# A hybrid diffusion trunk step on one core: layer 0's shift and scale modulation on 32-column tiles of TensorE, the gate sums moved among the Hyena projections, small loads on three queues

## The chip, the cores and the metric

One core of one Trainium2 chip runs the whole step in one launch. The metric is the device time of that launch in microseconds (us). Everything is computed in f32.

The engines are TensorE (PE; its weight loads are shown apart as PEld), VectorE (DVE), ScalarE (ACT), GpSimd (POOL) and SyncE (SP), which here only issues DMAs. ACT and POOL issue DMAs too, on queues of their own. A name such as SPq stands for the issuing side of an engine.

## What is computed

Two layers work on 640 tokens (512 latent tokens of one request, 128 context tokens of another), with a model width of 1024. Ahead of each layer stands the modulation that this change is about:

```
m = silu(cond) @ mod_w[i] + mod_b[i]          # cond: c or c_ctx, 1024 -> 3072
shift, scale, gate = split(m, 3)              # 1024 each
h = rms_norm(x, pre_norm_g[i]) * (1 + scale) + shift
x = x + gate * rms_norm(mixer(h), post_norm_g[i])
```

There are two conditioning vectors (`c` for latent tokens, `c_ctx` for context tokens), so that each layer multiplies two rows of 1024 by a matrix of 1024x3072. Shift and scale (columns 0 to 2047) are needed before the layer's input projection, the gate (columns 2048 to 3071) only after its output projection.

Layer 0's mixer runs a bidirectional gated DeltaNet (GDN) on one half of the channels and a Hyena long convolution on the other. The Hyena filters come from a small network (`hyena_ffn_w1`, `w2`, `w3`, with sines between) and are turned into spectra by matrix products with DFT tables. Layer 1 is attention; the change touches it only by where its modulation is computed.

## The kernel before

Every engine has a program written out by hand; each waits on semaphores. PSUM has 8 banks, used in a ring: each use is a numbered "fill", `FILLS` lists all of them in order, and fill f may be written when fill f-8 has been drained. `bank_full` counts fills that TensorE has completed, `bank_free` those that ScalarE or VectorE has drained.

**Weights.** All large weights come in chunks of 1024x256 (1 MB) into `wring`, which has `WSLOTS` = 3 slots. `chunk_list` gives the chunks in the order of their loads, `slot_of` the slot of each (before: chunk i in slot i mod 3), and SP issues them in that order (L563). It waits for each one's slot: chunk i may be loaded when the last fill computed with the chunk that had the slot before is full, which for a modulation chunk is the fill `mod_f` (below).

**Modulation.** A matrix of 1024x3072 is 12 chunks. Most chunks are summed on VectorE: `sum_modulation` (L1682, L1685) multiplies and adds the 8 row blocks of a chunk with the conditioning values as scalars, for both vectors: 16 instructions of 128x256. TensorE then adds over the 128 partitions with `modulation` (four products with a column of ones, 128x1), which makes the fill `mod_f`, and VectorE's `take_modulation` (L1696) adds the bias and drains it. Four of layer 0's chunks (1, 4, 7 and 10) go to TensorE alone: 16 products of 128x2. The sums have two places (`macc`).

**The stages around the change.**
1. Start: small loads on SP's queue (network weights, biases, frequencies, norm rows, `ident`), two layers of the filter network (TensorE, VectorE, ScalarE in turn), two transposes of the rows of vectors, SiLU of the conditioning.
2. Filters: 20 products of 128x512, each drained by VectorE.
3. Spectra: `spectrum` makes 24 fills with 42 products (L1102; two and two in 12 steps n), drained by ScalarE and VectorE (`take_spectra`). After each step n comes one modulation chunk of layer 0. ScalarE also squares and normalises x in the middle of this stage (L742, L793).
4. `turn_x` (L1199): x is transposed, and ScalarE (L803) and VectorE (L1751) apply scale and shift to it, into `hT`. For this all 12 chunks of layer 0 are needed, the gate's four included.
5. Hyena projections: eight times `project_cm` (`hy_f`, j = 0 to 7), each with one chunk of `even_in_w`: 16 products of 128x512 and 16 of 128x128. After each one from j = 1 on comes one modulation chunk of layer 1. ScalarE copies the result to `pad` (`take_rows`, L828), and VectorE's `convolve` (three taps) reads `pad` before the next may be copied there.
6. `tr_hy` (ten groups of four transposes, L1223, copied by VectorE at L1789), the DFT products `fft0`, and so on; then the six GDN projections `qkv_f` with five-tap convolutions. After q1, k0, k1, v0 and v1 stand the last five modulation chunks of layer 1.

## Time and profile before

| | |
|---|---|
| median of 3 runs | 1221.07 us (1217.9 to 1229.56) |
| the profiled execution's own time | 1225.3 us |
| its span, first to last instruction | 1223.5 us |
| mean granted TensorE clock over the span | 0.949 |
| TensorE busy | 1127.3 us (92%) |
| VectorE busy | 617.5 us (50%) |
| ScalarE, GpSimd busy | 308.0 us, 116.9 us |
| loads and stores | 78.99 MB |

The profiled execution is 4.2 us above the median of the runs. Start times in the rows count from the first instruction. Each f32 product stands in the trace as two records, so that "x8" at a `MATMUL` row is four products. The granted clock is 1.00 at 2.4 GHz and 0.50 at 1.2 GHz.

### The profile page before, as it was taken

The page shows a single profiled execution, that of the slowest core. Times are in us where ns is not written, and L with a number is a line of the kernel's source. Part 1 is how long each engine was busy: PE and PEld are TensorE (multiplying, and loading weights), DVE is VectorE, ACT ScalarE, POOL GpSimd, SP SyncE. Part 2 cuts the span into 40 slices and gives each one's busy share as a digit, 9 for nine tenths or more (in the row PEclk, how much of TensorE's full clock was granted, in tenths as well). Part 3 has the DMA queues.
Part 4 walks back from the last instruction along what each step waited for, and adds up shares of the span by engine and source line. Part 5 has one row for each costly group of instructions (what it writes and reads, how often), then busy time and mean ns, then how long its engine had stood idle before and what let it go on. Part 6 is the DMA issues. An engine that isn't in the chain of part 4 may idle for free.

```text
span 1223.5 us, 13372 instructions
## 1 busy us (share of the span) xinstructions
PE 1127.3 (92%) x5234; PEld 796.6 (65%) x5234; DVE 617.5 (50%) x1426; ACT 308.0 (25%) x751; POOL 116.9 (10%) x156
## 2 busy tenths in 40 slices
PE   3998999989899997899898889899999998999997
PEld 1456466567356555679698878788965655445686
DVE  3988235658396778856738810600028146333104
ACT  1064001000012135532121101611161356333212
POOL 2020000000120004110004300600000000010001
PEclk9997999998899898889899989899999999969999
DMA  8465142440010322010004111331221200000012
GB/s 272 127 205 174 35 132 75 137 136 2 1 35 18 126 72 70 1 35 1 1 1 138 50 72 35 96 95 61 69 69 45 70 1 0 1 1 1 1 35 86
DMA packets 68430, 78.99 MB, mean 65 GB/s; under 512 B 2606, under 2 KB 63518, under 8 KB 68368
## 3 DMA queue, kind: packets, MB, share of 16 engines
q1 hardware_dynamic: 64776, 69.54, 17.8%
q0 software_dynamic: 2304, 7.96, 2.1%
q8 instruction: 42, 0.69, 0.2%
q10 hardware_dynamic: 1288, 0.64, 0.2%
q14 instruction: 20, 0.16, 0.0%
HBM read 74.62 MB, written 3.51 MB: 64 GB/s over the span
## 4 chain that ended last, share of the span: by engine, by line
PE 73%; DVE 17%; ACT 4%; POOL 3%; issue 2%; DMA 1%; SPq 0%; POOLq 0%; DVEq 0%; ACTq 0%
PE ps L1102 69%; PE ps L1223 4%; DVE pad L1685 2%; DVE phase L1771 1%; DVE mix L1685 1%; DVE xreg L1771 1%; DVE xreg L2036 1%; DMA wring<-in_mod_w 1%; DVE phase L2044 1%; POOL stat L604 1%; DVE xreg L2058 1%; ACT phase L1072 1%; DMA phase<-in_hyena_sin_freq 1%; PE ps L1199 0%; DVE pad L1960 0%
## 5 line engine op out<-in xcount | busy, mean ns | idle before, releaser
L1102 PE MATMUL ps<-hT,wring 128*128 128x512 f32 (+2 forms) x1376 | 363.0, 425 | 2.3 <-ACT hT L803 2.3
L1102 PEld LDWEIGHTS ps<-hT,wring 128*128 128x128 f32 x1376 | 206.4, 192 | 157.5 <-issue 155.1
L1102 PE MATMUL ps<-phase 128*128 128x512 f32 (+4 forms) x518 | 173.3, 480 | 10.5 <-ACT phase L753 5.0
L1102 PE MATMUL ps<-wring,mix 128*128 128x256 f32 x640 | 140.2, 382 | 3.0 <-issue 2.2
L1102 PEld LDWEIGHTS ps<-phase 128*128 128x128 f32 (+2 forms) x518 | 86.8, 198 | 83.5 <-issue 67.1
L1102 PEld LDWEIGHTS ps<-wring,mix 128*128 128x128 f32 x640 | 122.5, 192 | 20.4 <-issue 2.6
L1102 PE MATMUL ps<-wring,hT 128*128 128x256 f32 (+1 forms) x480 | 100.4, 372 | 0.0
L1102 PEld LDWEIGHTS ps<-wring,hT 128*128 128x128 f32 x480 | 89.7, 192 | 10.6
L2084 DVE SCALAR_TENSOR_TENSOR phase<-phase,yst 128x1024 f32<-128x1024 f32 x10 | 12.9, 1287 | 124.2 <-POOL yst L604 124.2
L1223 PE MATMUL ps<-ident,phase 128*128 128x128 f32 x376 | 52.7, 297 | 20.2 <-DVE phase L1972 5.7
L1102 PE MATMUL ps<-hT,phase 128*128 128x64 f32 (+4 forms) x258 | 70.1, 408 | 0.8 <-DVE phase L1722 0.8
L1685 DVE SCALAR_TENSOR_TENSOR mix<-wring,scond,mix 128x256 f32<-128x256 f32 x168 | 67.5, 476 | 0.0
L1102 PE MATMUL ps<-xreg,phase 128*128 128x128 f32 (+1 forms) x420 | 57.2, 296 | 10.3 <-DVE xreg L2050 4.9
L1223 PEld LDWEIGHTS ps<-ident,phase 128*128 128x128 f32 x376 | 47.6, 155 | 26.7 <-issue 9.9
L1102 PEld LDWEIGHTS ps<-xreg,phase 128*128 128x128 f32 x420 | 49.4, 193 | 16.6 <-issue 9.2
L2099 DVE TENSOR_SCALAR ostat<-ostat 128x35 f32<-128x35 f32 x1 | 0.2, 180 | 109.6 <-ACT pad L997 109.6
L1102 PEld LDWEIGHTS ps<-hT,phase 128*128 128x128 f32 (+2 forms) x258 | 35.8, 196 | 27.5 <-issue 25.2
L962 ACT ACTIVATE phase<-ps 128x256 f32<-128x256 f32 x40 | 15.3, 382 | 122.0 <-PE ps L1102 122.0
L828 ACT ACTIVATE pad<-ps 128x512 f32<-128x512 f32 x24 | 14.1, 598 | 124.2 <-PE ps L1102 114.7
L1685 DVE SCALAR_TENSOR_TENSOR pad<-wring,scond,pad 128x256 f32<-128x256 f32 x112 | 44.9, 470 | 0.0
L1102 PE MATMUL ps<-mix,phase 128*128 128x64 f32 (+1 forms) x136 | 33.8, 418 | 5.4 <-DVE phase L1654 5.4
L2159 DVE TENSOR_REDUCE smax<-ps 128x1 f32<-128x512 f32 x32 | 22.0, 687 | 27.9 <-PE ps L1102 27.8
(302 smaller groups left out, 1247.0 us busy)
## 6 DMA issues: line engine op xcount, KB each, us to landing
wring<-in_mod_w SPq DMA_DIRECT2D x24, 1024.0 KB, 5.2
wring<-in_even_in_w SPq DMA_DIRECT2D x16, 1024.0 KB, 7.3
wring<-in_odd_in_w SPq DMA_DIRECT2D x9, 1024.0 KB, 5.2
wring<-in_even_out_w SPq DMA_DIRECT2D x4, 1024.0 KB, 7.4
wring<-in_odd_out_w SPq DMA_DIRECT2D x4, 1024.0 KB, 5.2
xreg<-in_x_sample SPq DMA_DIRECT2D x1, 2048.0 KB, 13.8
xreg<-in_x_sample POOLq DMA_DIRECT2D x1, 2048.0 KB, 8.0
out_y_sample<-xreg SPq DMA_DIRECT2D x4, 512.0 KB, 2.6
```

The lines of the kernel that those rows point to most:

```text
L604: nc.gpsimd.tensor_tensor(dst, src, eps[:, 2:3].broadcast_to([P, src.shape[1]]), ALU.pow)\
L828: nc.scalar.activation(pad[:, m, 2:2 + LS], bank(f + m), ACT.Copy).then_inc(free(f + m), 1)
L962: nc.scalar.activation(y[:, t, WC * j:WC * j + WC], bank(f)[:, 0:WC], ACT.Copy)\
L1072: nc.scalar.activation(prob[u % 2][:, g, 0:LS], bank(f + 1 + g), ACT.Exp, scale=scale, bias=nmax[:, u % 2, g:g + 1], accum_out=ssum[:, u % ...
L1102: return nc.tensor.matmul(o, l, r, start=first, stop=last)
L1223: ins = nc.tensor.transpose(bank(f)[:, h * P:h * P + P], src(h), idn)
L1685: ins = stt(o, w, sc, o, ALU.mult, ALU.add)
L1771: chained(stt(o, src, w, o, ALU.mult, ALU.add))
L2036: ins = stt(rr[:, d, h * P:h * P + P], bank(f)[:, h * P:h * P + P], sc(NEG, d, h), v_tm[:, tl[d], h * P:h * P + P], ALU.mult, ALU.add)
L2044: ins = stt(oh, bank(f)[:, h * P:h * P + P], sc(EG, d, h), oh, ALU.mult, ALU.add)
L2084: chained(stt(y[:, t, :], y[:, t, :], yst[:, 1, t:t + 1], gb_l[layer][:, 0 if t < TS else 1, :], ALU.mult, ALU.mult))
L2159: chained(nc.vector.tensor_reduce(smax[:, u % 2, 0, g:g + 1], bank(f + 1 + g), AXX, ALU.max))
```

## The change

- **Shift and scale of layer 0** (the first `EARLY` = 8 chunks) go to TensorE in another form. `gather_modulation`: the conditioning values stand as 32 columns (`scond_w`, 2 of them used, the others zero) and are the stationary operand; the chunk's 256 columns stream. The 8 row blocks go to four 32-column tiles of the array (`tile_position`), two to each. ScalarE copies the 128x256 result to `mrow`, and `turn_modulation` multiplies it with `pick` (128x2), which adds the four tiles and turns the row into columns. Gathers 0, 1 and 2 and turns 0 and 1 stand among the filter network's products, turn 2 and gather 3 between the two halves of the filters, turn 3 behind them, gathers 4 to 7 behind the spectra's steps n = 1, 3, 5 and 7, turns 4 to 7 behind n = 3, 5, 7 and 9.
- **The gate of layer 0** (4 chunks) and **all 12 chunks of layer 1** stay sums on VectorE. They stand behind the eight Hyena projections, 1, 2, 2, 2, 2, 2, 2 and 3 of them (`SUMS_AFTER`); the GDN projections have none.
- **Slots**: the first 8 chunks take the slots 0, 1, 2 in turn. In the Hyena stage all modulation chunks use slot 1, the projection weights slots 2 and 0 in turn. What a load waits for is as before.
- **Small loads**: the vectors' rows go to GpSimd's queue (ahead of the inverse DFT tables), the first layer's inputs, `ident` and the second layer's weights to ScalarE's, the frequencies and the conditioning to SP's. SP then loads chunks 0 and 1 ahead of the filter weights, 2 ahead of the DFT tables, 3 ahead of x.

```diff
+EARLY = 8
+SPEC_PAIRS = [("spec%d" % n, 2) for n in range(12)]
...
-SUMMED = [[j for j in range(12) if j not in (1, 4, 7, 10)], list(range(12))]
+SUMMED = [(0, j) for j in range(EARLY, 12)] + [(1, j) for j in range(12)]
+SUMS_AFTER = [1, 2, 2, 2, 2, 2, 2, 3]
...
+        mod_f = {}
+        for j in range(8):
+            for n in range(SUMS_AFTER[j]):
+                mod_f[SUMMED[len(mod_f)]] = hy_f[j] + 3 + n
...
+            for j in range(EARLY):
+                lst.append((mod[0], WC * j, WC, row_f[j]))
+            even_at = [columns + WC * half for columns in (HG0, HV0, HX10, HX20) for half in range(2)]
+            late = [(mod[layer], WC * j, WC, mod_f[layer, j]) for layer, j in SUMMED]
+            lst += [(even, even_at[0], WC, hy_f[0] + 2), late.pop(0), (even, even_at[1], WC, hy_f[1] + 2)]
+            for j in range(1, 8):
+                lst += [late.pop(0) for _ in range(SUMS_AFTER[j])]
+                if j < 7:
+                    lst.append((even, even_at[j + 1], WC, hy_f[j + 1] + 2))
...
-        slot_of = [i % WSLOTS for i in range(z1_at)] + [WSLOTS - 1, WSLOTS - 1]
+        slot_of = [i % WSLOTS for i in range(EARLY)]
+        evens = 0
+        for w, _, _, last in chunks[EARLY:z1_at - len(qkv_f)]:
+            if last in mod_f.values():
+                slot_of.append(1)
+            else:
+                slot_of.append((2, 0)[evens % 2])
+                evens += 1
...
+            def load_chunk(i):
+                w, c0, n, last = chunks[i]
...
+                earlier = [n_ for n_ in range(i) if slot_of[n_] == slot_of[i]]
+                if earlier:
+                    wait_full(sp, chunks[earlier[-1]][3])
+                sp.dma_start(wchunk(i)[:, :, 0:n], w[:, c0:c0 + n].rearrange("(k p) n -> p k n", p=P))\
+                  .then_inc(w_landed[slot_of[i]], 16)
...
+            take_sine(0)
+            take_modulation_rows(0)
+            take_sine(1)
+            for j in range(1, 4):
+                take_modulation_rows(j)
...
+            def gather_modulation(j):
+                f = row_f[j]
+                wait_free(pe, f)
+                pe.wait_ge(scond_ready, 4)
+                i = chunk_of[f]
+                wait_chunk(pe, i)
+                for k in range(KD):
+                    q = 32 * (k % 4)
+                    ins = nc.tensor.matmul(bank(f)[q:q + 32, 0:WC], scond_w[:, k, :], wchunk(i)[:, k, :],
+                                           start=k < 4, stop=k >= 4, tile_position=(0, q))
+                ins.then_inc(full(f), 1)
+            def turn_modulation(j):
+                f = col_f[j]
+                wait_free(pe, f)
+                pe.wait_ge(pick_ready, 1)
+                wait_drained(pe, row_f[j])
+                for m in range(2):
+                    ins = mm(bank(f)[:, 2 * m:2 * m + 2], mrow[j % 2][:, m * P:m * P + P], pick[:, :])
+                ins.then_inc(full(f), 1)
...
-                if n >= 1:
-                    modulation(0, n - 1)
-            modulation(0, 11)
+                if n in (3, 5, 7, 9):
+                    turn_modulation(4 + (n - 3) // 2)
+                if n in (1, 3, 5, 7):
+                    gather_modulation(4 + (n - 1) // 2)
...
                 project_cm(hy_f[j], chunk_of[hy_f[j] + 2])
-                if j >= 1:
-                    modulation(1, j - 1)
+                for n in range(SUMS_AFTER[j]):
+                    modulation(*SUMMED[sum(SUMS_AFTER[:j]) + n])
...
+            sum_modulation(*summed.pop(0))
+            for j in range(1, 8):
+                for _ in range(SUMS_AFTER[j]):
+                    sum_modulation(*summed.pop(0))
+                for _ in range(SUMS_AFTER[j - 1]):
+                    take_modulation(*taken.pop(0))
+                if j >= 3:
+                    convolve(hy_f[j - 1], 3, 60 + 4 * ((j - 3) // 2), 96 + 4 * ((j - 3) // 2),
+                             (cm[:, 0, :, :], cm[:, 1, :, :], hy_x2)[(j - 3) // 2], 2 * ((j - 3) % 2))
+            convolve(hy_f[7], 3, 60 + 8, 96 + 8, hy_x2, 2)
+            for which in taken:
+                take_modulation(*which)
+            gate_factors(0, mod_f[0, 11])
+            scale_factors(1, mod_f[1, 11])
+            gate_factors(1, mod_f[1, 11])
```

SP's queue in the Hyena stage. `in_mod_w` is a modulation chunk, `in_even_in_w` a projection's weights; `bank_full` followed by a bank's number is the wait for the fill that last used the chunk in that slot. Before:

```order
L563 DMA wring<-in_mod_w 128x8x256 [waits bank_full5]
L563 DMA wring<-in_even_in_w 128x8x256 [waits bank_full2]
L563 DMA wring<-in_mod_w 128x8x256 [waits bank_full5]
L563 DMA wring<-in_even_in_w 128x8x256 [waits bank_full6]
L563 DMA wring<-in_mod_w 128x8x256 [waits bank_full1]
L563 DMA wring<-in_even_in_w 128x8x256 [waits bank_full2]
```

And of the change, from the load of layer 0's chunk 8 (the first summed one) on:

```order
L550 DMA wring<-in_mod_w 128x8x256 [waits bank_full0]
L550 DMA wring<-in_even_in_w 128x8x256 [waits bank_full2]
L550 DMA wring<-in_mod_w 128x8x256 [waits bank_full7]
L550 DMA wring<-in_mod_w 128x8x256 [waits bank_full3]
L550 DMA wring<-in_even_in_w 128x8x256 [waits bank_full6]
L550 DMA wring<-in_mod_w 128x8x256 [waits bank_full4]
L550 DMA wring<-in_mod_w 128x8x256 [waits bank_full0]
```

Two modulation chunks now stand between two projection weights, and each waits for the bank that the modulation chunk just ahead of it fills.

TensorE behind Hyena projection 1; the first row is the projection's last group. `macc_ready` is VectorE's signal that a sum is complete, `w_landed` that a chunk has landed in the slot with that number. Before:

```order
L1102 MATMUL ps<-hT,wring 128x128 x15
L1102 MATMUL ps<-ones,mix 128x1 [waits macc_ready,bank_free6]
L1102 MATMUL ps<-ones,mix 128x1 x3
L1102 MATMUL ps<-hT,wring 128x512 [waits bank_free7,w_landed0]
L1102 MATMUL ps<-hT,wring 128x512 x7
```

And of the change:

```order
L1145 MATMUL ps<-hT,wring 128x128 x15
L1145 MATMUL ps<-ones,mix 128x1 [waits macc_ready,bank_free3]
L1145 MATMUL ps<-ones,mix 128x1 x3
L1145 MATMUL ps<-ones,mix 128x1 [waits macc_ready,bank_free4]
L1145 MATMUL ps<-ones,mix 128x1 x3
L1145 MATMUL ps<-hT,wring 128x512 [waits bank_free5,w_landed2]
```

One modulation fill stood between two projections and there are now two. The first is in bank 3, for which the fourth load of the list above waits, the second in bank 4, for which the sixth waits.

TensorE from the spectra's last steps to the transposes of x. `ones,pad` is a chunk summed on VectorE, `scond,wring` one on TensorE alone. Before:

```order
L1102 MATMUL ps<-hT,phase 128x512 x4
L1102 MATMUL ps<-ones,pad 128x1 x4
L1102 MATMUL ps<-hT,phase 128x512 x2
L1102 MATMUL ps<-ones,pad 128x1 x4
L1102 MATMUL ps<-hT,phase 1x512 x3
L1102 MATMUL ps<-scond,wring 128x2 x16
L1102 MATMUL ps<-ones,pad 128x1 x4
L1199 MATMUL ps<-ident,xreg 128x128 x40
```

And of the change, where `pick,pad` is `turn_modulation` and the 32x256 rows are `gather_modulation`:

```order
L1145 MATMUL ps<-hT,phase 128x512 x8
L1145 MATMUL ps<-pick,pad 128x2 x2
L1169 MATMUL ps<-wring,phase 32x256 x8
L1145 MATMUL ps<-hT,phase 128x512 x8
L1145 MATMUL ps<-pick,pad 128x2 x2
L1145 MATMUL ps<-hT,phase 128x512 x2
L1145 MATMUL ps<-hT,phase 1x512 x3
L1271 MATMUL ps<-ident,xreg 128x128 x40
```

A chunk stood behind every step and the last directly ahead of the transposes; now two turns and a gather stand here, and no product with ones.

## Rows read from the trace of the kernel before

**Rows 1.** The page: busy time by engine, and the chain that ended last by line
```profile
PE 1127.3 (92%) x5234; PEld 796.6 (65%) x5234; DVE 617.5 (50%) x1426; ACT 308.0 (25%) x751; POOL 116.9 (10%) x156
PE 73%; DVE 17%; ACT 4%; POOL 3%; issue 2%; DMA 1%; SPq 0%; POOLq 0%; DVEq 0%; ACTq 0%
```

**Rows 2.** The chain that ended last, 100 to 267 us: start, duration (us), what
```profile
100.93 5.15 DMA wring<-in_mod_w
106.10 0.62 DVE pad L1682 x2
106.72 5.55 DVE pad L1685 x14
...
112.40 1.75 PE ps L1102 x8
114.16 4.38 PE ps L1199 x20
118.56 4.30 ACT hT L803 x12
...
123.44 144.06 PE ps L1102 x560
```

**Rows 3.** Order of time on TensorE, 26 to 545 us: start, duration, line, names, records
```profile
26.84 19.27 PE L1102 MATMUL ps<-mix,phase 128*128 128x512 f32 x40 [5.42 <-DVE phase L1654]
...
99.95 0.95 PE L1102 MATMUL ps<-ones,pad 128*128 128x1 f32 x8
...
267.32 0.95 PE L1102 MATMUL ps<-ones,mix 128*128 128x1 f32 x8
268.13 1.65 PE L1223 MATMUL ps<-ident,xreg 128*128 128x128 f32 x12
...
277.74 15.62 PE L1102 MATMUL ps<-phase 128*128 128x512 f32 x36
...
364.95 1.89 PE L1102 MATMUL ps<-phase,xreg 128*128 128x256 f32 x8
...
399.38 1.84 PE L1102 MATMUL ps<-ones,mix 128*128 128x1 f32 x8 [3.95 <-DVE mix L1685]
401.08 20.01 PE L1102 MATMUL ps<-hT,wring 128*128 128x512 f32 x64
...
442.75 17.55 PE L1102 MATMUL ps<-hT,wring 128*128 128x512 f32 x64
...
471.38 3.43 PE L1102 MATMUL ps<-masks,phase 128*128 128x128 f32 x16 [6.26 <-DVE modc L1696]
...
501.21 2.79 PE L1223 MATMUL ps<-ident,phase 128*128 128x128 f32 x12 [5.19 <-DVE modc L1696]
```

**Rows 4.** SP's queue in order of time: start, duration of the issue, what
```profile
158.31 0.37 SPq L563 DMA_DIRECT2D wring<-in_mod_w  x1
159.10 0.37 SPq L563 DMA_DIRECT2D wring<-in_even_in_w  x1
```

**Rows 5.** VectorE in order of time, 160 to 180 us
```profile
163.67 0.61 DVE L1682 TENSOR_SCALAR mix<-wring,scond 128x256 f32<-128x256 f32 x2 [34.27 <-DMA wring<-in_mod_w]
...
176.94 0.61 DVE L1769 TENSOR_SCALAR xreg<-pad,vec 128x644 f32<-128x644 f32 x1 [7.12 <-ACT pad L830]
...
179.32 0.61 DVE L1769 TENSOR_SCALAR xreg<-pad,vec 128x644 f32<-128x644 f32 x1
```

**Rows 6.** Busy time in stretches: PE, PEld, DVE, ACT, POOL, granted clock, DMA share, GB/s
```profile
400.00:404.00 4.00, 4.00 (x10) 2.45 (x11) 3.86 (x6) 0.57 (x1) 0.00 (x0) 0.50 0.37 76
```

**Rows 7.** ScalarE in order of time, 68 to 87 us
```profile
68.68 0.60 ACT L776 ACTIVATE phase<-ps 128x512 f32<-128x512 f32 x1 [2.87 <-PE ps L1102]
...
86.44 1.05 ACT L766 ACTIVATE phase<-ps 128x512 f32<-128x512 f32 x2
```

**Rows 8.** Groups of instructions by line, 0 to 420 us
```profile
L1789 DVE COPY phase<-ps 128x512 f32<-128x512 f32 x10 | 6.1, 679 | 0.1
```

More of the change, by code:

```diff
@@ L431, in program @@
         qkv_f = [start[f"in_{c}{j}"] for c in "qkv" for j in range(2)]
-        spec_f, mod_f0 = spec_mod_fills(start["spec_mod"])
-        mod_f = [mod_f0, [f + 3 for f in hy_f[1:] + qkv_f[1:]]]
+        spec_f = [[start["spec%d" % (6 * o + j // 2)] + j % 2 for j in range(12)] for o in range(2)]
+        row_f = [start["row%d" % j] for j in range(EARLY)]
+        col_f = [start["col%d" % j] for j in range(EARLY)]
+        mod_f = {}
+        for j in range(8):
+            for n in range(SUMS_AFTER[j]):
+                mod_f[SUMMED[len(mod_f)]] = hy_f[j] + 3 + n
         inv_groups, sum_f, key_f = inverse_fills(start)
@@ L541, in _ @@
-            sp.dma_start(r2[96:108, :], a["hyena_conv_b"].rearrange("l (r c) -> (l r) c", c=P)).then_inc(rows_in, 16)
+                  .then_inc(film_col, 16)
+            r1 = rows[:, 0:128]
+            sp.dma_start(r1[80:88, :], a["c"].rearrange("l (r c) -> (l r) c", c=P)).then_inc(cond_in, 16)
+            sp.dma_start(r1[88:96, :], a["c_ctx"].rearrange("(r c) -> r c", c=P)).then_inc(cond_in, 16)
+            def load_chunk(i):
+                w, c0, n, last = chunks[i]
+                if last == start["out0"] + NT - 1:
+                    wait_full(sp, last_tr[-1])
+                earlier = [n_ for n_ in range(i) if slot_of[n_] == slot_of[i]]
[3 more added lines that the diff above has]
+                  .then_inc(w_landed[slot_of[i]], 16)
@@ L1129, in _ @@
                 .then_inc(full(f + 1), 1)
+            gather_modulation(0)
+            pe.wait_ge(sin_ready, 1)
+            pe.wait_ge(film2_in, 16 * 3)
+            f = start["film2"]
+            wait_free(pe, f)
+            mm(bank(f)[:, 0:LS], film_w[0:64, 128:256], h2[0:64, 0:LS]).then_inc(full(f), 1)
+            wait_free(pe, f + 1)
+            mm(bank(f + 1)[:, 0:LP], film_w[0:64, 128:256], h2[0:64, LS:TOK]).then_inc(full(f + 1), 1)
+            gather_modulation(1)
+            turn_modulation(0)
+            gather_modulation(2)
+            turn_modulation(1)
             pe.wait_ge(h2_ready, 1)
@@ L1654, in _, with take_modulation @@
             nc.vector.memset(h2[64:128, LS:LS + 1], 0.0).then_inc(h2_ready, 1)
+            def take_modulation(layer, j):
+                f = mod_f[layer, j] if (layer, j) in mod_f else col_f[j]
+                wait_full(dve, f)
+                tt(modc_l[layer][:, 2 * j:2 * j + 2, :], bank(f)[:, 0:4].rearrange("p (m c) -> p m c", m=2),
+                   vec1[:, 24 * layer + 2 * j:24 * layer + 2 * j + 2].unsqueeze(2).broadcast_to([P, 2, 2]),
+                   ALU.add).then_inc(free(f), 1)
+            take_modulation(0, 0)
+            take_modulation(0, 1)
             dve.wait_ge(tap_in, 16 * 7)
@@ L1691, in sum_modulation, with scale_factors @@
                             ins.then_inc(macc_ready, 1)
-            def take_modulation(layer, j):
-                f = mod_f[layer][j]
-                wait_full(dve, f)
-                tt(modc_l[layer][:, 2 * j:2 * j + 2, :], bank(f)[:, 0:4].rearrange("p (m c) -> p m c", m=2),
-                   vec1[:, 24 * layer + 2 * j:24 * layer + 2 * j + 2].unsqueeze(2).broadcast_to([P, 2, 2]),
-                   ALU.add).then_inc(free(f), 1)
-            def modulation_factors(layer, last):
+            def scale_factors(layer, last):
                 wait_drained(dve, last)
```

235 lines of the change are left out of this document (107 added, 128 removed).

## The prediction

> **What bounds the kernel now.** I read the page first, for busy times and the chain that ended last: TensorE is busy for 92% of the span and holds 73% of that chain, so time is won or lost where TensorE waits, or where it runs below its full clock [rows 1]. Then I read the chain in order of time up to the Hyena projections. It shows where TensorE is held by the modulation: between its products of one summed chunk, which end at 99.95 + 0.95 = 100.90, and those of another, which begin at 112.40, the chain runs through a load (5.15 us) and a sum on VectorE (0.62 + 5.55) [rows 2, 3]. From 123.44 on it is 144 us of TensorE without a break [rows 2]. The reader is to see in this that the Hyena stage has no wait to remove: one modulation chunk for each projection is loaded and summed behind it. Last I read TensorE in order of time in the GDN stage. There it waits three times behind VectorE: 3.95, 6.26 and 5.19 us [rows 3].
>
> **The start, filters and spectra.** The change takes VectorE's sums (8 chunks by about 6.2 us) and the four 128x2 chunks out of the spectra, and puts in gathers and turns. A product of 512 columns costs 15.62 / 18 = 0.87 us when TensorE is fed, one of 256 columns 1.89 / 4 = 0.45 to 0.47 [rows 3]. A gather is 8 products of 256 columns. At one after the other that is X = 3.6 us; if the four column tiles ran fully beside each other it would be a quarter, 0.9. The trace before has no tiled product; I take X = 2 and keep both ends. A turn is two small products, about 0.5 (half of the 0.95 for four).
> The start of the filters: the frequencies' load no longer gates TensorE, but ScalarE has two more table changes ahead of its sines, a gather may lie ahead of the second network product, and two chunks of 1 MB now stand ahead of the filter weights on SP's queue. I bound it by the 5.42 us that TensorE waits there now, all saved, and by one whole uncovered gather, 3.6 lost [rows 3]; I take +1.0, so 27.8.
> From there: filters 19.3, two turns 1.0, a gather X: 48.1 + X. Spectra to the end of step 4 are 18 products (15.6), two gathers and a turn: 64.2 + 3X. Here something new is late. ScalarE copies step 4's fill, squares and normalises x, and comes to the next copy 86.44 - 68.68 = 17.8 us later [rows 7]; before, VectorE's sums hid this. Turn 6, behind step 7, waits for ScalarE's copy of gather 6, so TensorE is not past it before 17.8 + 1.1 + 0.5 = 19.4 us: 83.6 + 3X. Then a turn, a gather, 13 products (11.3), a turn: the transposes of x begin at 95.9 + 4X = 103.9, against 114.16 [rows 2]. From them to the first projection it is 9.3 us now [rows 2]; ScalarE, with its last spectra copies no longer covered by a wait, adds some 1.3. So the first projection begins at 114.5 and not at 123.44: **-9** (-19 to +1).
> On X the Trainium skill speaks too. Its page "TensorEngine Tiling (Array Packing)", section "Overview" (Theoretical Speedup), has operands of at most 32 columns run up to four times faster, since the tiles work in parallel; by that X is 0.9 and the time 4 us lower than by X = 2. Its "Key Properties" say that a change of the tiling mode drains TensorE; each gather brings two such changes, and they would raise X. No row here shows either.
>
> **The Hyena stage: the wait that the change adds.** Now two modulation chunks stand behind each of projections 1 to 6, three behind the last, and all of them use slot 1. SP may load the second chunk of a pair only when TensorE has filled the bank of the first, and TensorE does this behind the projection. So the second chunk is not loaded, let alone summed, when TensorE wants it: TensorE finishes the first, then load, sum, and the second. Queued behind that waiting product on TensorE is the next projection; queued behind the waiting load on SP are the next projection's weights, which go out right after it and land during the sum. This is the very chain of [rows 2], with its price: 112.40 - 100.90 = 11.5 us. A projection's load queued 0.8 us behind does not stretch it: 158.31 to 163.67 is 5.4 for the load [rows 4, 5]. The first chunk of each pair costs nothing: it is loaded when the last pair is done and summed within 11.5 us, under a projection of (144.06 - 6 x 0.81) / 8 = 17.4 [rows 2]; the convolution, 2 x 2.38 = 4.8 [rows 5], also fits. Waits: one in each of six pairs, two in the last three: **8 x 11.5 = +92** (90 to 96).
> Products: 16 chunks instead of 7 on TensorE, nine more by 0.81 [267.32 to 268.13 in rows 3]: **+7**.
> Clock: after the wait at 395.4 the granted clock is 0.50, the lower level [rows 6], the four small products take 1.84 instead of 0.95 and the projection behind them 20.01 instead of 17.55: 3.4 us lost. After the wait of 5.19 the 12 records take 2.79 against 1.65: 1.1 lost [rows 3]. Each of the eight waits leaves TensorE idle for longer than these. I take 2.5 a wait, nearer to the row with a projection behind it: **+20** (9 to 27).
>
> **From the last chunk to the first DFT product.** Before, 268.13 to 277.74 = 9.6 us [rows 3]. Now VectorE comes from its last sum with two convolutions still to do: two small ones 0.3, convolution 4.8, ScalarE's copies 1.6, convolution 4.8, seven small ones 0.9, five copies by 0.61 [rows 8] = 3.0. Less the 1.1 by which the sum ends ahead of TensorE's products, 14.4: **+5** (3 to 7).
>
> **The GDN stage.** Five sums (6.2 each) leave VectorE, five fills leave TensorE and its ring. The three waits were 3.95 + 6.26 + 5.19 = 15.4 [rows 3]; the clock lost behind them is 3.4, 1.1 and, for the one at 471, 1.2 (3.43 for 16 records, against 16 x 1.65 / 12 = 2.2), together 5.7; the five fills are 4.1. In all 25.2. What is late next is VectorE: its convolutions still follow ScalarE's copies, and the last convolution stands ahead of the first key products' use. I take **-22** (-13 to -26).
>
> **The sum.** -9 + 92 + 7 + 20 + 5 - 22 = +93, against the profiled execution's own 1225.3: 1318. That execution is 4.2 above the median of the runs (1221.07), so the forecast for the median is **1314 us**. With every term at its low end the change is +68, with every term at its high end +124, so 1289 to 1345 for the median; they will not all fall to one side. What a measurement of this kernel can tell from no change is about 1%.
>
> **The rivals.**
> *The pairs are hidden* (faster). If the second load of a pair could run ahead of TensorE's first fill, by a free slot or by an order of SP's queue that I misread, two loads (10.4) and two sums (12.3) and a convolution (4.8) stand beside 19 us of TensorE: VectorE's 17.4 would just fit, and the 92 and the 20 go. Then -9 + 7 + 5 - 22 = -19: 1202. It decides at one point, whether a load can start before the fill of the chunk ahead of it. For it speaks that the stage has had no wait [rows 2]; against it that before, that fill was a slot two chunks back, and that the queue's order shows each load's wait for the bank of the chunk just ahead. 0.03.
> *The waits are there and the gains are not.* The eight waits come, but ScalarE's 17.8 and the gathers eat the start, X near 3.6 and the filters 3.6 later, and in the GDN stage VectorE stays the bound so that only 13 is won. Then +1 + 92 + 7 + 20 + 5 - 13 = +112: 1333. For it speaks that VectorE holds 17% of the chain [rows 1]. 0.10.
> *The clock stays low for longer.* If it did for the whole of each projection behind a wait, each lost another 14 us: 1314 + 7 x 14 = 1412 (the last wait has no projection behind it). Against it: at 401 the projection had lost only 2.5 [rows 3]. 0.02.
>
> **How the numbers follow.** The forecast has 0.85. The range takes its own bounds and most of the second rival: 1296 to 1336; I leave out about 2 in 10. Faster by over 1% is the first rival, 0.03; within 1% would need six of the eight waits to be missing, 0.01; slower by over 1% 0.96.
>
> **What would show it.** In the profile after: between two Hyena projections two groups of four products with ones, the second behind an idle time of some 11.5 us put down to VectorE's sum or its load, eight times in all; a modulation load issued within 0.1 us of the end of the first group; a granted clock near 0.50 at the start of each projection behind a wait; the first projection near 114; the first DFT product about 115 us later than now; no wait for VectorE behind q1 and v0. TensorE's busy share falls to some 87%. Projections that follow each other without such a gap would prove the forecast wrong.

## The result, and the profile after

| | before | after |
|---|---|---|
| median of 4 runs each | 1219.49 us (1216.43 to 1229.56) | 1314.10 us (1313.64 to 1323.22) |
| the profiled execution's own time | 1225.3 us | 1313.76 us |
| its span | 1223.5 us | 1311.7 us |
| mean granted TensorE clock | 0.949 | 0.920 |

The ratio is 1.077, with a 95% interval of 1.071 to 1.083: the changed kernel is slower by 94.6 us between the medians and by 88.5 between the profiled executions. The forecast was 1314.

The page of after, busy times, chain by engine, and two groups (columns: out<-in, count | busy us, mean ns of one | idle just before them and what ended it):

```profile
PE 1130.1 (86%) x5234; PEld 790.7 (60%) x5234; DVE 591.9 (45%) x1363; ACT 309.1 (24%) x761; POOL 118.8 (9%) x165
...
PE 69%; DVE 15%; ACT 5%; DMA 4%; POOL 2%; issue 2%; SPq 1%; POOLq 0%; ACTq 0%; DVEq 0%
...
L1145 PE MATMUL ps<-ones,mix 128*128 128x1 f32 x128 | 22.3, 296 | 92.0 <-DVE mix L1771 92.0
```

Against [rows 1], TensorE's busy time has hardly moved (1127.3 to 1130.1 us) while its share fell from 92% to 86%: on balance the time was added as idle time. (The lower clock behind the waits adds some 21 us of busy time, and about as much has gone elsewhere, among it the clock lost in the GDN stage, 5.7, and 9.7 us in the attention, for which see the last section.) The last row names the idle time. The products with ones, the second half of the modulation sums, stand behind 92.0 us of idle time, all of it put down to VectorE's sum.

TensorE of after in order of time, through the Hyena stage (start, duration, line, names, records, [idle before <- releaser]):

```profile
117.51 19.55 PE L1145 MATMUL ps<-hT,wring 128*128 128x512 f32 x64 [4.32 <-ACT hT L846]
...
155.09 0.95 PE L1145 MATMUL ps<-ones,mix 128*128 128x1 f32 x8
167.50 1.84 PE L1145 MATMUL ps<-ones,mix 128*128 128x1 f32 x8 [11.46 <-DVE mix L1771]
169.20 19.29 PE L1145 MATMUL ps<-hT,wring 128*128 128x512 f32 x64
188.33 0.95 PE L1145 MATMUL ps<-ones,mix 128*128 128x1 f32 x8
200.94 1.84 PE L1145 MATMUL ps<-ones,mix 128*128 128x1 f32 x8 [11.67 <-DVE mix L1771]
...
370.42 1.83 PE L1145 MATMUL ps<-ones,mix 128*128 128x1 f32 x8 [11.30 <-DVE mix L1771]
383.78 1.84 PE L1145 MATMUL ps<-ones,mix 128*128 128x1 f32 x8 [11.53 <-DVE mix L1771]
...
398.68 1.88 PE L1145 MATMUL ps<-phase 128*128 128x512 f32 x4
```

Where [rows 2] had one unbroken piece of 144 us, there are now eight waits: one in each of six pairs, at 167.50, 200.94, 234.69, 268.39, 302.39 and 336.52, and two in the last three sums. Together 11.46 + 11.67 + 11.62 + 11.39 + 11.47 + 11.53 + 11.30 + 11.53 = 91.97. The first DFT product stands at 398.68 and not at 277.74 [rows 3], 120.9 us later.

The first of these waits in the chain that ended last:

```profile
117.51 38.55 PE ps L1145 x144
156.05 0.02 issue
156.07 5.10 DMA wring<-in_mod_w
...
161.20 0.61 DVE mix L1768 x2
161.81 4.82 DVE mix L1771 x13
```

The reader is to see that this is the old chain of [rows 2], gate for gate: TensorE ends the first chunk of the pair at 156.04, SP's load starts 0.03 us later, then come the load, the sum and the second chunk's products. It was there once before, where TensorE had other products under most of it and idled 1.68 us in front of the sum's products; it is there eight times now, with nothing under it.

### The profile page after: what moved, and what is told of

Read it like the earlier page. It is cut to its first block, busy times and chain, and to the rows that moved or that the text cites. A ratio compares the mean times of both kernels' runs of the same rounds, so it can differ in the third digit from the quotient of the medians.

```text
span 1311.7 us, 13338 instructions
## 1 busy us (share of the span) xinstructions
PE 1130.1 (86%) x5234; PEld 790.7 (60%) x5234; DVE 591.9 (45%) x1363; ACT 309.1 (24%) x761; POOL 118.8 (9%) x165
## 4 chain that ended last, share of the span: by engine, by line
PE 69%; DVE 15%; ACT 5%; DMA 4%; POOL 2%; issue 2%; SPq 1%; POOLq 0%; ACTq 0%; DVEq 0%
PE ps L1145 65%; DMA wring<-in_mod_w 4%; DVE mix L1771 3%; PE ps L1295 3%; DVE phase L1849 1%; DVE xreg L2109 1%; DVE phase L2117 1%; POOL stat L620 1%; ACT hT L846 1%; PE ps L1169 1%; DVE xreg L2131 0%; ACT phase L1115 0%; POOL stat L619 0%; ACT phase L759 0%; DVE phase L1851 0%
## 5 line engine op out<-in xcount | busy, mean ns | idle before, releaser
L1145 PE MATMUL ps<-hT,wring 128*128 128x512 f32 (+2 forms) x1376 | 376.1, 436 | 5.2 <-ACT hT L846 4.3
L1145 PEld LDWEIGHTS ps<-hT,wring 128*128 128x128 f32 x1376 | 211.8, 196 | 168.8 <-issue 164.2
L1145 PE MATMUL ps<-phase 128*128 128x512 f32 (+4 forms) x522 | 169.7, 470 | 8.9 <-DMA phase<-k_pos_p 3.9
L1145 PE MATMUL ps<-ones,mix 128*128 128x1 f32 x128 | 22.3, 296 | 92.0 <-DVE mix L1771 92.0
L1771 DVE SCALAR_TENSOR_TENSOR mix<-wring,scond,mix 128x256 f32<-128x256 f32 x224 | 90.0, 477 | 0.0
L1145 PEld LDWEIGHTS ps<-ones,mix 128*128 128x128 f32 x128 | 22.0, 260 | 92.4 <-issue 92.4
L1768 DVE TENSOR_SCALAR mix<-wring,scond 128x256 f32<-128x256 f32 x32 | 9.8, 349 | 150.4 <-DMA wring<-in_mod_w 150.4
L871 ACT ACTIVATE pad<-ps 128x512 f32<-128x512 f32 x24 | 13.7, 595 | 261.2 <-DVE xreg L1851 157.8
L1145 PE MATMUL ps<-hT,phase 128*128 128x64 f32 (+4 forms) x258 | 65.2, 390 | 0.0
L1145 PEld LDWEIGHTS ps<-hT,phase 128*128 128x128 f32 (+2 forms) x258 | 34.7, 190 | 26.4 <-issue 24.0
```

Source lines behind the costliest of these rows:

```text
L871: nc.scalar.activation(pad[:, m, 2:2 + LS], bank(f + m), ACT.Copy).then_inc(free(f + m), 1)
L1145: return nc.tensor.matmul(o, l, r, start=first, stop=last)
L1771: ins = stt(o, w, sc, o, ALU.mult, ALU.add)
```

## The experiments

Each ran on one chip beside runs of the kernel before, and its ratio is to those. Unless an edit says otherwise it is made in the changed kernel. The edits are shown in part; "..." stands for lines left out.

### More slots for the modulation's chunks

The theory says that the waits come from slot 1 being the only one for the modulation. This edit gives it two more places, in memory that is free in this stage.

```diff
...
-                slot_of.append(1)
+                slot_of.append((1, 3, 4)[lates % 3])
+                lates += 1
...
+            return (wring[:, slot_of[i], :, :] if slot_of[i] < WSLOTS else
+                    view({3: 20992, 4: 18944}[slot_of[i]], KD, WC))
...
```

The first load into each new place also waits until that memory is free (for the last gather, and for ScalarE's squares).

> The change, but the sixteen summed modulation chunks rotate over three slots (slot 1 and two spaces in the phase buffer that are free in the Hyena stage), so that a load waits for a fill made a pair earlier. Theory (a load waits for TensorE's fill of the chunk just ahead): all eight waits of 11.5 us go (92.0) and with them the half-clock stretches behind them (20.8): 1314.1 - 92.0 - 20.8 = 1201 us, and no wait for VectorE longer than 1 us between projections. Rival (VectorE is too slow for two sums and a convolution in a projection, 17.4 of 19.0 us plus handovers): waits of 2 to 6 us stay in six gaps, 1215 to 1240 us. Rival (the bandwidth is short, three chunks in 19 us): TensorE waits for w_landed, 1215 us or more.

Measured: 1210.89 us (1207.25 to 1220.74), ratio 0.992 (0.988 to 0.996). TensorE in order of time:

```profile
139.85 17.55 PE L1150 MATMUL ps<-hT,wring 128*128 128x512 f32 x64
157.23 1.84 PE L1150 MATMUL ps<-ones,mix 128*128 128x1 f32 x16
...
271.79 1.84 PE L1150 MATMUL ps<-ones,mix 128*128 128x1 f32 x16
279.16 1.84 PE L1150 MATMUL ps<-ones,mix 128*128 128x1 f32 x8 [5.52 <-DVE mix L1776]
...
294.70 5.65 PE L1150 MATMUL ps<-phase 128*128 128x512 f32 x12
```

Both sums of a pair now stand in one group of 16 records, with no idle time before them, and every projection behind one takes 17.55. Seven of the eight waits are gone; the one left is at the third sum behind the last projection. The first DFT product comes 104.0 us earlier than in after. The sums stand in the same places on TensorE and only the slots differ, so the single slot makes these waits. The time came 10 us above its expectation, and up to the first DFT product it is 8.8 (104.0 gained, not 112.8). The rows have them: 5.52 + 0.89 for the wait that is left and the products behind it, 1.1 because the first projection starts later (118.61 against 117.51), 1.0 because it takes 20.58 and not 19.55, and 0.6 behind the sums. What the third sum costs in all is seen in the last experiment.

### The same three slots, in rotation

No memory is added; the order of slots is that of before (chunk i in slot i mod 3).

```diff
-            if last in mod_f.values():
-                slot_of.append(1)
-            else:
-                slot_of.append((2, 0)[evens % 2])
-                evens += 1
+            slot_of.append(len(slot_of) % WSLOTS)
...
```

> The change, with one line of slots as before it: every chunk of the Hyena stage takes the next of the three slots (two modulation chunks and one projection weight in turn). Theory (what counts is which fill a slot's load waits for): a pair is loaded during the projection ahead and costs nothing, but the next projection's weights wait for the end of this projection, land 5.2 to 7.4 us later and are covered by 1.6 us of small products: TensorE waits some 4 to 5 us at seven projections, 28 to 35, and loses some 2 us of clock at each: 1201 + 31 + 14 = about 1246 us. Rival (any two modulation chunks behind a projection cost the 11.5, whatever the slots): 1314 us.

Measured: 1257.54 us (1251.90 and 1263.19), ratio 1.028 (1.017 to 1.039).

```profile
188.04 19.06 PE L1141 MATMUL ps<-hT,wring 128*128 128x512 f32 x64 [4.33 <-DMA wring<-in_even_in_w]
...
323.13 1.84 PE L1141 MATMUL ps<-ones,mix 128*128 128x1 f32 x8 [9.79 <-DVE mix L1767]
```

The wait moves from the sum to the next projection's weights, as expected, and costs 4.3 to 4.5 us instead of 11.5, since no sum on VectorE follows the load. Three chunks to a projection with three slots leave no slot free for the next weights. There are six such waits, not the seven expected (26.4 us and not 31), and the 9.79 in front of the last sum wasn't foreseen. With 0.89 for the clock behind it, that is some 6 us more than expected, which is what the lower of the two times shows (1251.90 against 1246); the higher has the 10 us of the last section besides.

### Half of each sum

Only every second of a chunk's 8 row blocks is loaded into the sum on VectorE.

```diff
-                for k in range(KD):
+                for k in range(0, KD, 2):
...
```

> The change, with VectorE's sums over four of the eight row blocks only (the other four are left out of the modulation's sums): a sum takes 3.1 instead of 6.2 us. Theory (each wait is load plus sum): each of the eight waits falls from 11.5 to 8.4, 1314.1 - 8 x 3.1 = 1289 us. Rival (the waits hang on the load alone, and the sum is hidden): 1314 us.

Measured: 1298.09 us (1297.34 and 1298.84), ratio 1.061 (1.051 to 1.071).

```profile
164.78 1.84 PE L1145 MATMUL ps<-ones,mix 128*128 128x1 f32 x8 [8.46 <-DVE mix L1771]
166.48 19.60 PE L1145 MATMUL ps<-hT,wring 128*128 128x512 f32 x64
```

The eight waits are 8.23 to 8.53 us, 3.1 shorter: the sum stands in each wait at its full length. Up to the first DFT product (374.13) the kernel gained 24.6 us, which is what 8 x 3.1 gives. Of these the profiled execution kept 16.4, and the time is 9 us above the 1289 expected; its profile has the long attention stage of the last section.

### The waits filled with products that nobody reads

In front of each of the eight waiting sums TensorE makes 12 products of 128x512, whose results nobody uses, so that it doesn't stand still.

```diff
                 wait_free(pe, f)
+                if nth in (2, 4, 6, 8, 10, 12, 14, 15):
+                    for _ in range(12):
+                        mm(bank(f), idn, hT[:, 0, 0:LS])
                 pe.wait_ge(macc_ready, 2 * nth + 2)
```

> The change, with twelve products of 128x512 (of the identity and a block of hT, into the bank that the modulation fill overwrites; they add nothing to the result) ahead of each of the eight waits. They take about 10.5 us at the full clock, inside the 11.5 of the wait. Theory (the 20.8 us behind the waits are the clock that falls while TensorE idles): the waits stay 11.5 us from fill to fill, the projections behind them take 17.5 and not 19.3 to 20.1, the four small products 0.95 and not 1.84: 1314.1 - 20.8 = 1293 us. Rival (the slower projections come from sharing memory with the load that lands then): 1314 us, projections stay near 20.

Measured: 1304.25 us (1297.44 to 1309.07), ratio 1.065 (1.058 to 1.073).

```profile
155.18 0.95 PE L1145 MATMUL ps<-ones,mix 128*128 128x1 f32 x8
155.99 10.55 PE L1145 MATMUL ps<-hT,ident 128*128 128x512 f32 x24
167.46 1.05 PE L1145 MATMUL ps<-ones,mix 128*128 128x1 f32 x8 [0.92 <-DVE mix L1774]
168.38 17.55 PE L1145 MATMUL ps<-hT,wring 128*128 128x512 f32 x64
```

The second sum starts 12.3 us after the first in both kernels (155.18 to 167.46 here, 155.09 to 167.50 in after [12.4]), so the wait is as long as it was. But its products take 1.05 and not 1.84 us, and four of the six projections behind such a wait take 17.55 instead of 19.3 to 20.1 (the other two 19.25). From the start of the first projection to the first DFT product it is 265.25 us against 281.17: 15.9 less, though TensorE had more to do. This separates the clock's share from the waits' own. The rival, that projections are slow because a load lands beside them, is excluded: the same loads land beside the four that take 17.55. The granted clock is 1.00 in the first 3.6 us of the one at 168.38, and 0.56 and 0.65 in the first 4 us of the two that take 19.25, behind waits of 1.04 and 2.06. The time expected was 1293; the four times are 1297.44, 1299.89, 1308.61 and 1309.07, and the gap between their pairs is the 10 us of the last section.

### The gathers in one tile

All 8 products of a gather go to the same 32 columns of the array.

```diff
...
-                    ins = nc.tensor.matmul(bank(f)[q:q + 32, 0:WC], scond_w[:, k, :], wchunk(i)[:, k, :],
-                                           start=k < 4, stop=k >= 4, tile_position=(0, q))
+                    ins = nc.tensor.matmul(bank(f)[0:32, 0:WC], scond_w[:, k, :], wchunk(i)[:, k, :],
+                                           start=k == 0, stop=k == KD - 1, tile_position=(0, 0))
...
```

The copy and the turn then take only this tile's 32 rows; a turn takes 0.60 us instead of 0.50.

> The change, with all eight products of a gather in the same 32 columns of the array, so that none can run beside another (the turn takes the one tile's rows; the sum is the same). Theory (the four tiles run beside each other, eight products of 128x256 in 1.00 us at the full clock): a gather takes about 3.5 us at the full clock, 2.5 more each; five of the eight stand on the path and one of them lies in turn 6's wait, so about 4 x 2.5 = +10: 1324 us. Rival (it is the 32-column operand alone that is fast): a gather stays at 1.0 and the time at 1314.

Measured: 1327.41 us (1324.36 to 1336.71), ratio 1.088 (1.081 to 1.095). One gather and what follows it, here and then in after:

```profile
47.17 3.64 PE L1168 MATMUL ps<-wring,phase 128*32 128x256 f32 x16
50.75 8.85 PE L1145 MATMUL ps<-mix,phase 128*128 128x512 f32 x20
```

```profile
43.75 1.07 PE L1169 MATMUL ps<-wring,phase 128*32 128x256 f32 x16
44.75 1.56 PE L1145 MATMUL ps<-mix,phase 128*128 128x512 f32 x3
```

In one tile the next product starts 3.58 us after the gather, in four tiles 1.00 us after it. So X, which the prediction took as 2 between 0.9 and 3.6, is 1.0. By the Trainium skill, page "TensorEngine Tiling (Array Packing)", section "Overview" (Theoretical Speedup), operands of up to 32 columns can run up to four times faster. The trace agrees: it is 3.6 times. By the Trainium skill, the same page, section "Key Properties", a change of the tiling mode drains TensorE. The trace leaves little room for it: if both forms pay the same d for their two changes and four tiles take a quarter of the rest T, then d + T = 3.58 and d + T / 4 = 1.00, which makes d 0.14 us (an estimate).

The first projection came at 131.40, 13.9 us later than in after: 4.7 of it stand ahead of the filters (37.86 against 33.15), where two of the three gathers take 6.2 and 6.1 us, and 9.2 from there on. The expectation of +10 counted only the latter. Tiling is worth its place.

### The third chunk ahead of the filter weights

In the changed kernel the load of chunk 2 stands behind the filter weights and other small loads on SP's queue; here it goes out right behind chunk 1.

```diff
             load_chunk(1)
+            load_chunk(2)
...
-            load_chunk(2)
```

> The change, with modulation chunk 2 loaded ahead of the filter weights and window, not behind them. Theory (the filters' start at 33.15 hangs on the bytes ahead of them on SP's queue in any order): gather 2 runs at once, but the filter weights land some 3 us later and GpSimd's negation with them, so that the filters start within 1 us of 33.2 and the time stays at 1314. Rival (chunk 2 alone is what is late): the filters start near 30, 3 us sooner, 1311 us.

Measured: 1322.54 us (1315.22 to 1328.80), ratio 1.084 (1.075 to 1.093). First TensorE here, then GpSimd in after:

```profile
25.63 1.94 PE L1169 MATMUL ps<-wring,phase 128*32 128x256 f32 x16 [3.12 <-DMA wring<-in_mod_w]
...
37.00 10.38 PE L1145 MATMUL ps<-mix,phase 128*128 128x512 f32 x20 [8.49 <-POOL mix L614]
```

```profile
27.40 2.79 POOL L614 TENSOR_SCALAR mix<-mix 64x1024 f32<-64x1024 f32 x1 [17.07 <-DMA phase<-in_hyena_bias]
```

Neither side had this. The gather comes 4.8 us earlier (30.41 in after), but the filters start at 37.00 instead of 33.15. They need the filter weights after GpSimd's pass over them, which in after ends at 30.2, just ahead of chunk 2's gather. Two paths end within some 3 us of each other there, and pulling one forward on a shared queue pushes the other back: GpSimd's pass starts at 33.95 here, 6.6 us later. The profiled executions differ by 4.0 us (1317.76 and 1313.76), and the filters' starts by 3.85.

### Before, without the modulation in the GDN stage

In the kernel before, the last five modulation chunks of layer 1 are left out of projections, loads and sums; their columns are set to 0.5.

```diff
...
-                    if j >= 1:
+                    if j >= 1 and fills is hy_f:
                         lst.append((mod[1], WC * taken, WC, mod_f[1][taken]))
...
-                if j >= 1:
-                    modulation(1, 6 + j)
...
```

> The kernel before, without the five modulation chunks of the GDN stage: their loads, sums, products and takes are left out (those columns of layer 1's modulation are a constant instead). Theory (the GDN stage of the change is 25.5 us shorter because of this alone): 1219.5 - 25.5 = 1194 us, with no wait of TensorE for VectorE behind q1 and v0. Rival (a part of it comes from what else moved, the fills and slots): 1194 + 5 to + 12.

Measured: 1195.74 us (1192.35 to 1206.64), ratio 0.981 (0.973 to 0.988). From the first DFT product to the first product of the chunk stage (`phase,wring`, 128x64) it is:

```profile
280.32 4.03 PE L1102 MATMUL ps<-phase 128*128 128x512 f32 x9
...
514.80 7.09 PE L1102 MATMUL ps<-phase,wring 128*128 128x64 f32 x32 [1.72 <-ACT phase L919]
```

That is 234.48 us. In after it is 633.14 - 398.68 = 234.46, in before 537.69 - 277.74 = 259.95. Freeing the GDN stage of the modulation gives 25.5 us, and nothing else of the change acts there to within 0.02.

### A better version: ScalarE's normalisation later, and two sums everywhere

Two steps on top of the kernel with more slots. In the first, ScalarE normalises x behind its copy of gather 6 instead of ahead of it, so that turn 6 no longer waits for it:

```diff
                 if o == 0:
                     for t in range(NT):
                         square_x(0, t)
-                    for t in range(NT):
-                        act.wait_ge(rstd_ready, t + 1)
-                        nc.scalar.activation(x[:, t, :], x[:, t, :], ACT.Copy, scale=stat[:, 1, t:t + 1])\
-                            .then_inc(xn_ready, 1)
...
                         take_modulation_rows((4, None, 6, 7)[2 * o + kt])
+                        if o == 1 and kt == 0:
+                            for t in range(NT):
+                                act.wait_ge(rstd_ready, t + 1)
...
```

> As e1, and ScalarE normalises x (five instructions, 5.3 us) not between the two orders of spectra but behind its copy of gather 6, which turn 6 waits for. Theory (turn 6 waits 7.1 us for ScalarE's 17.8 us of work): the wait falls to about 2, the first projection starts some 5 us earlier, and the time is 5 below that of e1, 1196 us. Rival (TensorE waits for ScalarE later in the same measure, at the transposes of x): the same time as e1.

Measured: 1200.78 us over three executions (1199.70 to 1201.54), ratio 0.983 (0.976 to 0.989). A fourth, the profiled one, took 2299.31 us; it is left out of the ratio and told of in the last section. So no trace shows this step by itself; turn 6's wait is read from the next one. The time is 5 us above the 1196 expected and 10 below that of the kernel with more slots, 5 having been expected of the step.

In the second, the sums behind the eight projections are spread evenly:

```diff
-SUMS_AFTER = [1, 2, 2, 2, 2, 2, 2, 3]
+SUMS_AFTER = [2, 2, 2, 2, 2, 2, 2, 2]
...
```

> The kernel of e5 with two sums behind each of the eight projections, the first among them, in place of 1, 2, 2, 2, 2, 2, 2, 3. In e1 the only wait left at a sum was the 5.52 us in front of the third one behind the last projection. Theory: with no third one there that wait is gone and no other comes, since VectorE has the first two chunks' sums done before the first projection ends: the first DFT product comes 5 to 6 us sooner after the first projection's start than in e1 (there 176.1 us after it, so here 170 to 171), and the time is near 1196. ScalarE's wait before the sixth turn (7.12 us in the changed kernel) is under 2 us. Rival: the chunk of W that the second projection needs comes behind one chunk of the modulation more in SP's queue, so that a wait of 3 us or more stands before the second projection or before its pair, and the time is 1199 to 1203, no better than e5.

Measured: 1186.55 us (1185.90 to 1198.35), ratio 0.975 (0.966 to 0.984). This beats both kernels, by some 34 us and 128 us.

```profile
87.23 0.58 PE L1151 MATMUL ps<-pick,pad 128*128 128x2 f32 x4 [1.95 <-ACT pad L789]
...
110.77 18.99 PE L1151 MATMUL ps<-hT,wring 128*128 128x512 f32 x64 [4.32 <-ACT hT L852]
...
131.30 17.55 PE L1151 MATMUL ps<-hT,wring 128*128 128x512 f32 x64
...
263.25 1.84 PE L1151 MATMUL ps<-ones,mix 128*128 128x1 f32 x16
...
272.19 15.72 PE L1151 MATMUL ps<-phase 128*128 128x512 f32 x36 [1.14 <-DVE phase L1880]
```

Turn 6 waits 1.95 us (7.12 in after), and the first projection starts at 110.77, 7.8 us ahead of the kernel with more slots. No wait is left at any sum. From the first projection to the first DFT product it is 161.4 us and not 176.1. The expectation had 170 to 171: the even spread gave 14.7, not 5 to 6, and 14.0 of it lie behind the last group of two sums. Between the last group of two sums and the first DFT product it was 22.9 us (271.79 to 294.70) and is 8.9 (263.25 to 272.19), and the reason stands on VectorE. With more slots, then here:

```profile
272.86 0.62 DVE L1773 TENSOR_SCALAR mix<-wring,scond 128x256 f32<-128x256 f32 x2 [6.87 <-PE ps L1150]
...
290.60 6.06 DVE L1878 COPY phase<-ps 128x512 f32<-128x512 f32 x10
```

```profile
251.29 0.61 DVE L1774 TENSOR_SCALAR mix<-wring,scond 128x256 f32<-128x256 f32 x2
...
269.06 6.07 DVE L1880 COPY phase<-ps 128x512 f32<-128x512 f32 x10
```

The third sum of three had its chunk, but waited 6.87 us for TensorE: the sums have two places (`macc`), and the third needs the place of the first, which TensorE reads only behind the last projection. Behind it on VectorE stand the convolutions and the copies of the transposes, all late with it; the copies begin 18.8 us after the start of TensorE's last group of two sums there (271.79), and 5.8 us after it here (263.25). That expectation counted only the wait that TensorE's row showed, and not the work queued behind the instruction waited for.

## Why the prediction was right, point by point

**The waits.** Forecast 8 x 11.5 = 92, measured 91.97, in the eight places named. The price was right because it was not estimated: it was read off the same chain where the kernel before had it once [rows 2]. More slots remove it, a rotation moves it to the weights and halves it, and a shorter sum shortens it.

**The clock.** Forecast +20, as 8 x 2.5. The eight groups behind a wait take 1.84 instead of 0.95 us, 7.1 in all, and the six projections behind one take 19.29, 19.63, 19.83, 20.04, 20.11 and 20.11 instead of 17.55, 13.7 in all: 20.8. Granted clock in after, columns as in [rows 6]:

```profile
167.00:169.00 2.00, 1.50 (x8) 1.53 (x8) 0.42 (x2) 0.00 (x0) 0.00 (x0) 0.50 0.00 0
...
173.00:177.00 4.00, 4.00 (x10) 1.71 (x9) 2.41 (x7) 0.00 (x0) 0.00 (x0) 1.00 0.20 67
```

After the idle 11.46 us the clock is at the lower level, 1.2 GHz, and from 173.00 on, 3.8 us after the projection's start, it is at 2.4 GHz. Keeping TensorE busy in the waits made this stage 15.9 us shorter: this term is shown too. The rival by which the clock stays low for the whole of a projection is excluded by the last row; its price also counted seven projections behind a wait where there are six.

**Products.** Forecast +7 for nine chunks more at 0.81. At full clock this is what they take.

**The start.** Forecast -9 (first projection at 114.5), measured -5.9 (117.51). Two steps were off and partly balanced. The filters start at 33.15 and not at 27.8, 5.35 late. The prediction bounded this by [rows 3] alone, at worst by one gather of 3.6, and didn't lay out SP's queue. One issue there held SP for 4.36 us (0.37 to 0.58 is what the issues of [rows 4] and those behind the pairs took), chunk 2's load took 15.38 us to land where those in the eight waits take 5.0 to 5.3, and gather 2, which stands ahead of the filters, waited 8.98 us for it:

```profile
10.15 4.36 SPq L560
...
14.90 15.38 DMA wring<-in_mod_w
```

```profile
30.41 1.93 PE L1169 MATMUL ps<-wring,phase 128*32 128x256 f32 x16 [8.98 <-DMA wring<-in_mod_w]
```

Against this X was 1.0 and not 2, 4 us over the four gathers between the filters' start and the transposes. With X = 1 the forecast's own steps give 72.1 us from the filters' start to the transposes (105.3 with the late start), and it is 74.2: 2.1 came back. The lower clock is among it, since behind the waits the first ten filter products take 10.33 instead of 8.85 us, the gather behind turn 6 1.93 instead of 1.07 and the eight products behind that 9.22 instead of 7.13. These are 4.4 us, so other steps had been counted some 2 too long. The wait of turn 6 for ScalarE came as foreseen:

```profile
71.41 0.60 ACT L819 ACTIVATE phase<-ps 128x512 f32<-128x512 f32 x1 [0.58 <-PE ps L1145]
...
89.16 1.05 ACT L805 ACTIVATE phase<-ps 128x512 f32<-128x512 f32 x2
```

These are 17.75 us, and the forecast from [rows 7] was 17.8. One loss was missed: the first projection itself takes 19.55 instead of 17.55, as it stands behind a wait of 4.32.

**The tail.** Forecast +5, measured 398.68 - 385.48 = 13.2 against 9.6: +3.6. From the end of the last sum on VectorE to the first DFT product it is 15.05 us where the forecast had 15.4; the other 0.8 us are the last products with ones, which take 1.84 us at the lower clock, so that the sum ends 1.9 us ahead of them and not 1.1.

**The GDN stage.** Forecast -22, measured -25.5, and the run that frees only this stage gives the same to 0.02 us. The allowance of 3 for a late VectorE, which had no row behind it, wasn't needed: the three waits are gone in after, and the longest of TensorE for VectorE from the first DFT product to the chunk stage is 0.88 us. In before, the waits with their clock and the five fills were the whole cost, as the 25.2 worked out for them says.

**The sum.** Up to the first product of the chunk stage, after is 95.4 us behind before. The profiled executions differ by 88.5 only. The missing 7 are no effect of the change, see the last section: with the attention stage at equal clock the difference would be some 98, which is 5 more than the forecast's 93. These 5 are the start (+3.1) and the first projection (+2.0), the clock (+0.8), the tail (-1.4), the GDN stage (-3.5), 2.5 between the GDN and the attention stage and under 2 of rest. Of the rest, 1.1 is that a group of four small products lasts 0.95 us in front of each of the eight waits and not the 0.81 to the next product's start. The 2.5 are not shown to be an effect of the change: that stretch takes 519.5 us in before and 521.9 in after, but 519.1 and 519.9 in the profiles of the half sum and the even spread. So the total of 94.6 between the medians agrees with the forecast of 93 to 2 us, closer than its terms do: the mechanism was right, and the last microseconds are luck.

The bounds were added up wrongly: the terms' low ends make +64 and their high ends +125, not +68 and +124. The stated range, 1296 to 1336, is narrower than either.

**The rivals.** "The pairs are hidden" stood at 1202 on one point: whether a load can start before the fill ahead of it. In the changed kernel it can't; with more slots it can, and the kernel comes to 1210.9. So the point was named rightly, and 1202 was somewhat low, for the third sum's wait. "The waits are there and the gains are not" is excluded by the start (-5.9) and the GDN stage (-25.5).

## What to carry to other kernels

When work moves between stages, count the buffers at the new place: a ring that gave each load a lead of two uses gives none when all loads of a kind share one slot, and two uses in a row then pay the whole chain of load and sum. Find that chain where the old kernel already has it and multiply it; then look at what is queued behind the instruction waited for, since that work comes late too. Here the idea was good (25 us from the GDN stage, a few from the start), one line of slot numbers cost 104, and with slots and an even spread the same idea is 2.5% faster than before.

## What the runs showed of the hardware that I had not expected

**A stretch at the lower clock that comes in some executions.** In the attention stage, in code that no experiment touches, the two records of a product of 512 columns take 2.07 us in one profile and 1.12 in another, at the same place of the program. Before, then after:

```profile
1083.29 2.07 PE L1102 MATMUL ps<-phase 128*128 128x512 f32 x2
...
1099.32 6.05 PE L1102 MATMUL ps<-phase,hT 128*128 128x512 f32 x10
```

```profile
1180.59 1.12 PE L1145 MATMUL ps<-phase 128*128 128x512 f32 x2
...
1189.02 4.56 PE L1145 MATMUL ps<-phase,hT 128*128 128x512 f32 x10
```

The granted clock there (20 us from 1077 in before, from 1175 in after) is 0.62 and 1.00, though TensorE is busy for 19.45 of the 20 us in both. TensorE's last idle time before it is the same too, 0.56 and 0.55 us. From one place in the attention (the product at 1057.16 in before, at 1155.08 in after) to the end of the span it is 166.3 us in the profiles of before and of the first four experiments (slots, rotation, half sum, filled waits), and 156.6 in those of after, of one tile, of the third chunk first, of the freed GDN stage and of the even spread: the two differ by 9.7 us and nothing lies between. The single times fall apart in the same way: of 31 runs of the kernel before, 21 lie between 1215.8 and 1221.4 and 10 between 1225.5 and 1234.2. What sets it off stays open. For reading: compare profiles stage by stage, or 10 us of this are taken for an effect. It is why half a sum gained 24.6 us in its stage and 16.4 in the profiled total, and why before's profiled execution lay above its median.

**One execution at half speed with a granted clock of 1.00.** The profiled execution of the kernel with the later normalisation took 2299.31 us, its three others 1199.70 to 1201.54. Its projections take over twice the usual 17.55 us, though the granted clock of its rows is 1.00:

```profile
213.23 37.63 PE L1151 MATMUL ps<-hT,wring 128*128 128x512 f32 x64
```

Why stays open. On a small scale the same is seen in the one-tile run, where the gather at 14.08 takes 6.18 us and the one at 21.46 takes 3.64, with a granted clock of 1.00 from 14 to 20 us. For reading: hold the granted clock against the duration of a product that is known from another profile.

**Four column tiles at f32** run beside each other almost fully: 1.00 us against 3.58 for the same 8 products of 256 columns.
